# Two transformer blocks in fp32 on one core: the layer norm's order and engines, and the weight panels' split and buffers, are changed

## What is computed

```python
x = layer_norm(ALPHA * x + part(x), g, b)
# layer_norm: mu = mean(x); var = mean((x - mu)**2)
#             (x - mu) * rsqrt(var + 1e-5) * g + b
```

## Time and profile before

| | |
|---|---|
| time, median of 3 runs | 3352.04 us (3347.63 to 3352.54) |
| span of the profiled execution | 3337.5 us, 35573 instructions |
| PE busy | 3085.6 us (92%) |
| POOL busy | 1602.5 us (48%) |
| DVE busy | 1279.3 us (38%) |
| ACT busy | 600.1 us (18%) |
| DMA | mean 80 GB/s, 262.40 MB read |

### The profile page before, as it was taken

How to read it: one execution, slowest core, us unless ns; L and a number is a source line. 1 busy time by engine, 2 the same in 40 slices (tenths; PEclk the granted TensorE clock), 3 DMA queues, 4 the chain that set the end, 5 groups by cost and what they waited for, 6 DMA issues and landing times.

```text
span 3337.5 us, 35573 instructions
## 1 busy us (share of the span) xinstructions
PE 3085.6 (92%) x15212; PEld 2562.8 (77%) x15212; DVE 1279.3 (38%) x1524; ACT 600.1 (18%) x1257; POOL 1602.5 (48%) x552
## 2 busy tenths in 40 slices
PE   7968999899989897998999899888999998989998
PEld 7856778788778666787887787777887876778876
DVE  2445422522137395125321311834332067543312
ACT  1214212110001161121110011451010022411100
POOL 3620283465555402834655445423655544546553
PEclk8989999999999998999999989999999998899999
DMA  3310141233222201412232222001332221022322
GB/s 122 101 63 32 46 150 52 89 100 101 89 89 95 76 1 51 148 55 89 89 100 91 92 84 93 1 14 63 101 101 90 100 95 63 26 88 89 101 89 75
DMA packets 182494, 266.79 MB, mean 80 GB/s; under 512 B 6592, under 2 KB 145984, under 8 KB 182336
## 3 DMA queue, kind: packets, MB, share of 16 engines
q1 hardware_dynamic: 173664, 241.19, 21.9%
q10 hardware_dynamic: 8672, 23.32, 2.0%
HBM read 262.40 MB, written 2.10 MB: 79 GB/s over the span
## 4 chain that ended last, share of the span: by engine, by line
PE 79%; DVE 12%; POOL 4%; issue 2%; ACT 1%; DMA 1%; DVEq 0%; ACTq 0%; POOLq 0%
PE PS L447 22%; PE PS L449 22%; PE PS L448 22%; PE PS L749 3%; POOL wlo L2057 3%; DVE x_row L646 2%; PE PS L1472 2%; PE PS L532 2%; PE PS L735 1%; DVE x_row L650 1%; POOL whi L2055 1%; DVE x_row L638 1%; PE PS L1296 1%; PE PS L881 1%; DVE stats L641 1%
## 5 line engine op out<-in xcount | busy, mean ns | idle before, releaser
L2055 POOL TENSOR_SCALAR whi<-raw 128x2048 fp32r<-128x2048 f32 x230 | 444.9, 1934 | 1568.1 <-PE PS L449 1555.1
L2057 POOL TENSOR_TENSOR wlo<-raw,whi 128x2048 fp32r<-128x2048 f32 x230 | 1070.1, 4653 | 19.2
L447 PE MATMUL PS<-xT_hi,whi 128*128 128x512 f32 (+1 forms) x2304 | 855.5, 371 | 24.3 <-POOL wlo L2057 24.1
L448 PE MATMUL PS<-xT_lo,whi 128*128 128x512 f32 (+1 forms) x2304 | 847.0, 368 | 0.0
L449 PE MATMUL PS<-xT_hi,wlo 128*128 128x512 f32 (+1 forms) x2304 | 846.8, 368 | 0.0
L447 PEld LDWEIGHTS PS<-xT_hi,whi 128*128 128x128 f32 x2304 | 440.3, 191 | 102.9 <-issue 14.0
L448 PEld LDWEIGHTS PS<-xT_lo,whi 128*128 128x128 f32 x2304 | 440.1, 191 | 72.1 <-issue 2.2
L449 PEld LDWEIGHTS PS<-xT_hi,wlo 128*128 128x128 f32 x2304 | 439.3, 191 | 70.1
L924 DVE TENSOR_TENSOR htmp<-sil,PS 128x512 f32<-128x512 f32 x88 | 56.5, 684 | 640.8 <-ACT sil L909 640.8
L447 PE MATMUL PS<-whi,h_hi 128*128 128x512 f32 x704 | 275.9, 392 | 10.0 <-DVE h_lo L930 10.0
L447 PE MATMUL PS<-whi,xT_hi 128*128 128x512 f32 x672 | 269.6, 401 | 12.8 <-ACT d_xs L1339 8.0
(11 more groups left out here) (375 smaller groups left out, 3599.6 us busy)
## 6 DMA issues: line engine op xcount, KB each, us to landing
raw<-ffn_w SPq DMA_DIRECT2D x66, 1024.0 KB, 5.0
raw<-ffn_w_gu SPq DMA_DIRECT2D x44, 1024.0 KB, 5.0
raw<-ffn_w_down SPq DMA_DIRECT2D x22, 1024.0 KB, 4.9
raw<-mem_wkv SPq DMA_DIRECT2D x16, 1024.0 KB, 5.2
raw<-even_w_in SPq DMA_DIRECT2D x14, 1024.0 KB, 5.2
raw<-ev_w_in SPq DMA_DIRECT2D x14, 1024.0 KB, 5.3
raw<-odd_w_in SPq DMA_DIRECT2D x12, 1024.0 KB, 5.1
raw<-od_w_in SPq DMA_DIRECT2D x10, 1024.0 KB, 5.2
```

Of the source, the lines that this page charges most:

```text
L447: pe.matmul(o, lhs[0], rhs[0], start=start, stop=False, skip_group_check=True)
L448: pe.matmul(o, lhs[0], rhs[1], start=False, stop=False, skip_group_check=True)
L2055: pool.tensor_scalar(whi[b][:, :], raw[b][:, :], 1.0, 1.0, ALU.mult, ALU.mult).then_inc(panel_hi, 1)
L2057: pool.tensor_tensor(wlo[b][:, :], raw[b][:, :], whi[b][:, :].bitcast(F32), ALU.subtract)\
```

## The change

Four edits, which are independent of each other except where said.

Buffers: three of `raw` and of `whi`; `wlo` lies in the memory of `raw`, so the low half is written over the loaded panel. A load waits for PE to be done with the panel three back; the split waits for the load alone.

```diff
+NB = 3
-        raw = [place(f"raw{i}", "raw", 4 * PANEL * i, [P, PANEL]) for i in range(2)]
-        wlo = [place(f"wlo{i}", "lo", 4 * PANEL * i, [P, PANEL], F32R) for i in range(2)]
+        raw = [place(f"raw{i}", "raw", 4 * PANEL * i, [P, PANEL]) for i in range(NB)]
+        wlo = [place(f"wlo{i}", "raw", 4 * PANEL * i, [P, PANEL], F32R) for i in range(NB)]
...
-                if n >= 2:
-                    sp.wait_ge(panel_split, n - 1)
+                if n >= NB:
+                    sp.wait_ge(*panel_done[n - NB])
```

```diff
-                pool.wait_ge(panel_loaded[b], 16 * (n // 2 + 1))
-                if n >= 2:
-                    pool.wait_ge(*panel_done[n - 2])
-                pool.tensor_scalar(whi[b][:, :], raw[b][:, :], 1.0, 1.0, ALU.mult, ALU.mult).then_inc(panel_hi, 1)
-                pool.wait_ge(panel_hi, n + 1)
-                pool.tensor_tensor(wlo[b][:, :], raw[b][:, :], whi[b][:, :].bitcast(F32), ALU.subtract)\
-                    .then_inc(panel_split, 1)
+                pool.wait_ge(panel_loaded[b], 16 * (n // NB + 1))
+                for q in range(2):
+                    cs = slice(1024 * q, 1024 * q + 1024)
+                    pool.tensor_scalar(whi[b][:, cs], raw[b][:, cs], 1.0, 1.0, ALU.mult, ALU.mult).then_inc(panel_hi, 1)
+                for q in range(4):
+                    cs = slice(512 * q, 512 * q + 512)
+                    if q % 2 == 0:
+                        pool.wait_ge(panel_hi, 2 * n + q // 2 + 1)
+                    m = pool.tensor_tensor(wlo[b][:, cs], raw[b][:, cs], whi[b][:, cs].bitcast(F32), ALU.subtract)
+                m.then_inc(panel_split, 1)
```

```diff
-            pool_at.append(len(panels) + 1)
+            pool_at.append(len(panels) + 2)
...
             def pool(pool):
+                pool.wait_ge(proj_ready, jobs[-1].ready)
```

```diff
             finish(0)
             finish(1)
-            if head:
-                turn(0)
             add(0, 3).then_inc(panel_used, 1)
             finish(2)
             if head:
-                turn(1)
+                turn(0)
             finish(3)
             if head:
-
+                turn(1)
                 head(pe, lambda: (turn(2), turn(3)))
...
+            def deviation(t):
+                act.wait_ge(mean_ready, base + t + 1)
+                act.activation(ln_sq[:, :], x_row[:, t, :], ACT.Square, bias=nmean[:, t:t + 1],
+                               accum_out=vsum[:, t:t + 1]).then_inc(var_ready, 1)
                 act.wait_ge(var_ready, base + t + 1)
+                act.activation(std[:, t:t + 1], vsum[:, t:t + 1], ACT.Sqrt, scale=1.0 / D, bias=eps_col[:, 0:1])\
+                    .then_inc(std_ready, 1)
+            deviation(0)
+            deviation(1)
+            if head:
+                act_turn(act, xT_hi, 0, KD, 0, 0)
+            deviation(2)
+            if head:
+                act_turn(act, xT_hi, 0, KD, 2, 1)
+            deviation(3)
...
+            def centre(t):
+                xt = x_row[:, t, :]
                 dve.wait_ge(y_ready, base + t + 1)
+                step(dve.scalar_tensor_tensor(out=xt, in0=xt, scalar=ALPHA, in1=two_banks(t), op0=ALU.mult, op1=ALU.add,
+                                              accum_out=zsum[:, t:t + 1]))
+                dve.tensor_scalar(nmean[:, t:t + 1], zsum[:, t:t + 1], -1.0 / D, None, ALU.mult).then_inc(mean_ready, 1)
+                dve.wait_ge(mean_ready, base + t + 1)
+                step(dve.scalar_tensor_tensor(out=two_banks(t), in0=xt, scalar=nmean[:, t:t + 1], in1=ln_gb[:, 0, :],
+                                              op0=ALU.add, op1=ALU.mult))
+            def finish(t):
+                dve.wait_ge(std_ready, base + t + 1)
+                step(dve.reciprocal(rstd[:, t:t + 1], std[:, t:t + 1]))
+                dve.scalar_tensor_tensor(out=x_row[:, t, :], in0=two_banks(t), scalar=rstd[:, t:t + 1], in1=ln_gb[:, 1, :],
                                          op0=ALU.mult, op1=ALU.add).then_inc(row_ready, 1)
+            centre(0)
+            centre(1)
+            finish(0)
+            finish(1)
+            centre(2)
+            if head:
+                dve_turn(dve, xT_hi, xT_lo, 0, KD, 0, 0)
+            else:
+                finish(2)
+            centre(3)
+            if head:
+                dve_turn(dve, xT_hi, xT_lo, 0, KD, 2, 1)
+                finish(2)
+            finish(3)
```

More of the change, by code:

```diff
@@ L66, in build @@
         at["raw"] = at["W"] + 98304
-        at["hi"] = at["raw"] + 2 * 4 * PANEL
-        at["lo"] = at["hi"] + 2 * 4 * PANEL
-        at["lnrow"] = at["lo"] + 2 * 4 * PANEL
+        at["hi"] = at["raw"] + NB * 4 * PANEL
+        at["lnrow"] = at["hi"] + NB * 4 * PANEL
         at["par"] = at["lnrow"] + 2 * 4 * D
@@ L99, in build @@
         xT_lo = place("xT_lo", "X", 4 * KD * S, [P, KD, S], F32R)
[L100 to L102 removed]
+        raw = [place(f"raw{i}", "raw", 4 * PANEL * i, [P, PANEL]) for i in range(NB)]
+        whi = [place(f"whi{i}", "hi", 4 * PANEL * i, [P, PANEL], F32R) for i in range(NB)]
+        wlo = [place(f"wlo{i}", "raw", 4 * PANEL * i, [P, PANEL], F32R) for i in range(NB)]
         ln_gb = place("ln_gb", "lnrow", 0, [P, 2, D])
@@ L105, in build @@
         small = Area("small")
-        stats = small("stats", [P, 12])
-        mv = small("mv", [P, NT, 2])
+        zsum = small("zsum", [P, NT])
+        nmean = small("nmean", [P, NT])
+        vsum = small("vsum", [P, NT])
         std = small("std", [P, NT])
@@ L129, in build @@
         h_lo = w("h_lo", [P, NF, S], F32R)
+        ln_sq = place("ln_sq", "W", w.off, [P, D])
         sil = w("sil", [P, 2, S])
@@ L250, in build @@
         assert w.off <= 4 * (8 + 4 + 4 + 4 + 4 + 4 + 4 + 2) * S
-        panel_loaded = [sem(f"panel_loaded{i}") for i in range(2)]
+        panel_loaded = [sem(f"panel_loaded{i}") for i in range(NB)]
         panel_hi = sem("panel_hi")
@@ L442, in next_panel @@
             pe.wait_ge(panel_split, used[0])
-            return [(whi[k % 2], wlo[k % 2]) for k in range(first, first + n)]
+            return [(whi[k % NB], wlo[k % NB]) for k in range(first, first + n)]
         def product(pe, o, lhs, rhs, start, stop):
@@ L634, in dve_block_out, with two_banks @@
             dve.wait_ge(*ln_loaded)
-            for t in range(NT):
+            def two_banks(t):
+                return PS[:, 2 * t:2 * t + 2, :].rearrange("p a b -> p (a b)")
+            def centre(t):
+                xt = x_row[:, t, :]
                 dve.wait_ge(y_ready, base + t + 1)
[L637 to L647, removed]
+                step(dve.scalar_tensor_tensor(out=xt, in0=xt, scalar=ALPHA, in1=two_banks(t), op0=ALU.mult, op1=ALU.add,
[4 more added lines that the diff above has]
+                                              op0=ALU.add, op1=ALU.mult))
@@ L2037, in _ @@
             for n, src in enumerate(panels):
-                if n >= 2:
-                    sp.wait_ge(panel_split, n - 1)
+                if n >= NB:
+                    sp.wait_ge(*panel_done[n - NB])
                 nk = src.shape[1]
-                sp.dma_start(raw[n % 2][:, :].rearrange("p (k c) -> p k c", k=nk), src).then_inc(panel_loaded[n % 2], 16)
+                sp.dma_start(raw[n % NB][:, :].rearrange("p (k c) -> p k c", k=nk), src).then_inc(panel_loaded[n % NB], 16)
+            for t in range(NT):
+                sp.wait_ge(row_ready, NT * (len(code) - 1) + t + 1)
+                sp.dma_start(out[128 * t:128 * t + 128, :], x_row[:, t, :]).then_inc(stored, 16)
+            sp.wait_ge(stored, 16 * NT)
         @block.gpsimd
```

20 lines of the change are left out of this document (2 added, 18 removed).

## The result

| | before | after |
|---|---|---|
| time, median | 3349.99 us (4 runs) | 3263.22 us (4 runs, 3260.61 to 3270.33) |
| ratio | | 0.9742, interval 0.9730 to 0.9753 |
| span of the profiled execution | 3337.5 us | 3268.5 us |
| PE busy / idle within the span | 3085.6 / 251.9 us | 3071.0 / 197.5 us |
| DVE, ACT, POOL busy | 1279.3, 600.1, 1602.5 us | 932.2, 649.4, 1750.0 us |

The kernel is 86.8 us faster. The direction and the new wait came as worked out, the size did not.

A forecast was written before the change was run, and what follows sets the result against it. PE taken as the bound, busy 3085.6 of 3337.5 us; 36 + 4 + 10 + 4.2 + 4 + 4.4 - 0.7 - 0.4 = 61.5 off 3352.0 gave 3290 us. Own range 3272 to 3306; with rivals 3267 to 3324.

The forecast's parts named there:

- Two become one, worth 1 us where both show, but a slow stretch follows the new one: Half-clock stretches after PE's long stalls at stage boundaries: the seven boundaries taken as 36 us for a net 34.
- `cross`: Two stages where PE follows POOL panel by panel: three buffers bring panels 2 us earlier each, 4 together (bounds -8 and 14).
- `odd`: RoPE stage: split in pieces, POOL delays DVE's `L1383` less; PE's 8.0 us wait falls to 3.8, gaining 4.2.
- `lru`: DVE-paced last 44 us hold 12 us of port losses; pieces gain 4 us of PE's 10.4 waits (bounds -2 and 10).
- tail: Final layer norm after the last product: DVE's four tiles take 17.8 us for 22.2, gaining 4.4.
- Boundaries and `h_lo`: Seven boundaries gain 36 us despite a new 4.3 us `xT_lo` wait each; `h_lo` waits at four down products go, 10.0.
- POOL's share in `hgrn`: POOL's first share in `hgrn`, moved behind one more panel, comes 0.4 us late.
- POOL keeping the port through its pieces: Rival 1: queued pieces hold the port, so boundaries, RoPE and `lru` gain nothing; 3335 us, chance 0.08.
- Table loads between Square and root: Rival 2: layer norm's Square and square root need different ACT tables; 23 us back, 3313 us, chance 0.05.
- The gap elsewhere: Rival 3: full DVE moves the head by 2 to 4 us at seven boundaries; 3318 us, chance 0.10.
- POOL as the bound of every panel: Rival 4: slower if pieces make a panel outlast PE's 10.85 us; at 11.5, 3414 us; chance 0.07.
- the four terms: Gains from splitting in pieces: down product 10.0, RoPE in `odd` 4.2, `lru` 4, the start -0.7 us.

The follow-up runs named there:

- first pair: Profiled executions of the kernel before and the changed kernel, as first measured: spans 3337.5 and 3268.5 us.
- second pair: Kernel before and changed kernel profiled and timed once more, neither edited: 3350.42 us (ratio 1.0002) and 3265.36 us (ratio 0.9747).
- turned order: Changed kernel with tile 1's transpose, rounding and low half right behind tile 0's, before DVE centres tiles 2 and 3: 3219.51 us, ratio 0.9620.

## Why the prediction was off in size and right in kind

**Around the span: wrong.** The forecast was put together from the profiled span and a median 14.5 us above it, with "what lies around the span as unchanged". That part is 1.8 us. Of the 25.3 us by which the gain was underrated, 10.7 are the distance of before's profiled execution from its median (3350.0 - 3339.3), 7.1 that of after's (3270.3 - 3263.2), and 7.5 lie between the profiles (69.0 for 61.5).

**PE's busy time: the mis-sized term.** The sum held 59.5 us of idle time, and 2 for the clock. Found were 54.4 and 55.0 idle in the two pairs, and 14.6 and 20.7 less busy time: seven and ten times the term. If the idle part holds in every run, the medians leave 86.8 - 55 = 32 us for the busy part; that was not measured by itself.

"Two become one, worth 1 us where both show, but a slow stretch follows the new one" was not where the clock's gain came from. Before, the clock is below full speed in two stretches of this boundary:

```profile
590.00:600.00 10.00, 7.78 (x33) 6.64 (x34) 8.66 (x12) 1.27 (x3) 2.37 (x2) 0.83 0.01 2
...
610.00:620.00 10.00, 5.38 (x40) 4.94 (x39) 9.76 (x12) 1.26 (x3) 0.73 (x1) 0.94 0.33 107
620.00:630.00 10.00, 10.00 (x77) 10.00 (x76) 1.35 (x3) 2.37 (x3) 0.00 (x0) 0.89 0.32 105
```

After, it is so in one:

```profile
600.00:610.00 10.00, 5.86 (x31) 5.36 (x30) 8.82 (x13) 3.69 (x8) 10.00 (x8) 0.75 0.34 106
610.00:620.00 10.00, 10.00 (x80) 10.00 (x80) 0.27 (x1) 1.46 (x4) 5.52 (x5) 0.91 0.01 2
```

The shares that the clock lacks are 0.17 + 0.06 + 0.11 of 10 us before, and 0.25 + 0.09 after: 3.4 us both times. Two short stretches became one of the same total length. What did fall in every `ffn` stage is the number of PE's waits, from six to one. An estimate from the earlier trace rows: the 0.50 us of a matmul behind a wait against the steady 0.226 make 0.27 us of busy time for each wait, 5 x 0.27 = 1.4 us for this stage, and its busy time did fall by 1.4. Over the kernel PE has 119 waits of over 0.15 us before (117 in the second profile) and 86 (88) after; by the same estimate they are worth 9 and 8 us. The other 6 and 13 us are left for the granted clock, and that has room for them. Span and mean clock make 254 and 229 us at 1.2 GHz in the first pair, 267 and 222 in the second; half of the difference, 12 and 22 us, is the most that the clock can be worth, less what lies where PE is idle.

**Stage by stage**, from the first tile's sums of one boundary to those of the next, us gained:

| | `even` | 2 `cross` | 4 `ffn` | `odd` | `hgrn` | `lru` | tail | sum |
|---|---|---|---|---|---|---|---|---|
| forecast | -0.7 | 4.0 | 30.6 | 9.3 | 4.7 | 9.1 | 4.4 | 61.4 |
| of it idle time | -0.7 | 4.0 | 29.4 | 9.1 | 4.5 | 8.9 | 4.4 | 59.6 |
| first pair of profiles | -5.5 | 4.8 | 39.4 | 4.6 | 4.1 | 15.5 | 5.9 | 69.0 |
| of it idle / busy | -1.8 / -3.7 | 0.1 / 4.7 | 30.5 / 9.0 | 6.4 / -1.8 | 6.8 / -2.8 | 6.4 / 9.2 | 5.9 / 0 | 54.3 / 14.6 |
| second pair | -5.6 | 5.2 | 39.4 | 7.7 | 8.1 | 15.0 | 5.9 | 75.7 |
| of it idle / busy | -0.1 / -5.5 | 0.2 / 5.1 | 30.5 / 8.9 | 7.1 / 0.6 | 5.2 / 2.9 | 6.3 / 8.7 | 5.9 / 0 | 55.1 / 20.7 |
| turned order | -5.4 | 10.6 | 62.7 | 10.0 | 11.9 | 23.2 | 5.9 | 119.0 |

(Each stage but `cross` and the tail has one boundary in it, 5.1 us in the forecast, and each `ffn` 2.5 for `h_lo`.)

- Boundaries and `h_lo`: right in mechanism. 9.3 us of waits became 4.14 (4.3 forecast), `h_lo` went. Each `ffn` lost 7.6 us of idle time, for 7.4 in the sum; the further 1.4 to 3.5 of each is busy time.
- `cross`: the number is right (2.4 to 2.8 each, for 2), by luck. It was to come from PE's waits for POOL's panels, but the idle time is the same as before: what those waits and the one for `x_row` gave, the wait of 4.2 us for `xT_lo` took, which the forecast did not have in front of the memory's panels. The gain is all busy time. The turned order, without that wait, gains another 3.0 and 2.8 us.
- `odd`: the wait for `d_xs` fell to 3.6 as forecast (3.8), but not by the pieces alone, to which the forecast put it down: it is 5.1 with the pieces alone and 3.6 with the buffers alone. In the changed kernel with whole splits the stage lost 8.3 us, so the pieces bring 13 there. In that kernel the splits stand in front of other steps of the rotation: up to 5.04 us for one that takes 0.69 us undisturbed. The stage gave 6.4 and 7.1 us of idle time for 9.1, and its busy time went up by 1.8 in one pair and down by 0.6 in the other; what takes the rest is open.
- `hgrn`: 6.8 and 5.2 us of idle time for 4.5, but busy time up by 2.8 in one pair and down by 2.9 in the other.
- `lru`: 15.5 and 15.0 for 9.1, but not from the port. Its idle time fell by 6.4, for 8.9; the two waits of the earlier trace rows fell by only 2.1 (10.4 us to 5.7 + 2.6). The other 9.2 us are busy time, at a granted clock that rose from 0.90 to 0.94 over the stage. Here the clock was the largest single thing that the sum lacked.
- `even`: -0.7 was forecast for the later first split, and PE's wait for it grew by just that (8.17 to 8.86). -5.5 came, and -5.6 in the second pair. Most of it is PE's busy time, 3.7 and 5.5 us more, at a clock of 0.91 and 0.90 for 0.92. The other kernels have between 0.0 (layer norm and pieces) and -6.8 (layer norm alone, 6.5 of it busy time), and no one part goes with it. Why the slow stretches of this stage get longer stays open.
- Tail: 5.9 for 4.4. DVE ends 17.4 us after the last boundary's first sums, near the 17.8 of the forecast (whose own terms, 4 x 4.25 and two waits of 0.6, make 18.2), and from there to the end of the span it is 3.0 us for 4.2, which had been left at nothing.
- POOL's share in `hgrn`: the 0.4 us was too small to see.

The lower end of the range, 3267, was called half of the bounds that were left, but 12 and 6 are the whole distances (48 - 36, 10 - 4) and only the 5 of `cross` is a half. With all three whole it would have been 3262, just below the time.

**The rivals.** POOL keeping the port through its pieces: refuted by the 1.56 us row; had it held, the pieces could not have brought 43 us where they did. Table loads between Square and root: refuted, there are nine for 40 roots, as before:

```profile
L621 ACT ACTIVATE std<-vsum,eps_col x40: 294/295/297, 406.9 to 3263.6; 128x1 f32<-128x1 f32 x40
L621 ACT ACT_TABLE_LOAD x9: 1283/1283/1283, 405.6 to 3250.7; - x9
```

The gap elsewhere: at the seven heads it returned as the one forecast wait and not beyond it; the two into `cross` were not foreseen. POOL as the bound of every panel: refuted, 7.4 us a panel against 10.85, and no wait for `wlo` is left outside `cross` and the start. The Trainium skill's page "SBUF — State Buffer" (section "Who interferes with whom") left open who goes first when POOL has a piece queued; by its silence the four terms could have been as small as 10. The waits of three of them fell by 10.0, 4.4 and 2.1, 16.5 together. The 3.41 and 4.75 us rows show what it does say: the lock lasts a whole instruction, so the length of the other engine's instructions is the price.

## What to carry to other kernels

Where several engines meet at a stage boundary, parts of a change are not worth their sum: look for what is late next before dropping one that brings nothing alone. Price a stall with what the clock takes after it: here waits of 3.5 us cost four tenths of their length again, waits of 1.1 us did not. The producer that the next stage's first matmul needs goes first on its engine, ahead of work for later tiles. Split what a stage gained into idle and busy time before calling a term right: here `cross` came out right for another reason, and `lru` came out larger by the clock alone. Take the base of a sum from more than one execution: a single profile lay 11 us from its kernel's median, with no change in the code.

## What the runs showed of the hardware

- A sum on the side of an instruction is a second, short instruction: 0.08 us on DVE behind the 1.22 us addition, 0.185 on ACT. A Square of 1024 columns with a bias and a sum took 1.152 us, where the activation of the earlier trace rows took 1.044.

```profile
L618 ACT ACTIVATE ln_sq<-x_row,nmean x40: 1147/1152/1157, 404.4 to 3262.3; 128x1024 f32<-128x1024 f32 x40
L618 ACT ACTIVATION_READ_ACCUMULATOR ln_sq<-x_row,nmean x40: 182/185/201, 405.4 to 3263.4; 128x1 f32 x40
```

- Splitting an instruction costs POOL little: 4 x 1.323 us in the mean for 4.605, with the waits for DVE's turns in it; undisturbed, four pieces took 5.02 us at 652.15.
- Writing to PSUM does not free a DVE instruction of the port while both its inputs are in SBUF (3.41 and 4.75 us for 1.29); the low halves, with one input in PSUM, took 0.679 to 0.694 us in all 124 cases.

```profile
L553 DVE TENSOR_TENSOR xT_lo<-PS,xT_hi x124: 679/681/694, 11.6 to 2909.0; 128x512 fp32r<-128x512 f32 x124
```
